# Expert weights in one transfer a tile, with runs of 8 KB for a partition

## What is computed

```python
y = jnp.zeros(xt.shape, dtype=jnp.float32)
for e in range(N_EXPERTS):                                  # 16
    he = jax.nn.silu(xt @ w_gate[e]) * (xt @ w_up[e])       # 1024 -> 512
    y = y + combine[:, e:e + 1] * (he @ w_down[e])          # 512 -> 1024
```

## Time and profile before

| | |
|---|---|
| median of 3 runs | 2187.03 us (2185.16 to 2195.76) |
| span of the profiled execution, its own time | 2187.5 us |
| TensorE busy (matmul) | 1962.1 us, 90% |
| weight loads busy | 1488.9 us, 68% |
| VectorE, ScalarE, GpSimd busy | 746.8, 737.2, 1008.6 us |
| mean granted TensorE clock | 0.944 of full |
| bytes moved by DMA | 477.02 MB, mean 218 GB/s |

### The profile page before, as it was taken

The page is one execution under the profiler, slowest core; times in us unless marked ns, Lnnn a source line. Parts: engine busy times, 40 slices in busy tenths (PEclk is TensorE's granted clock), DMA queues, the critical chain, the costliest instruction groups (busy, mean ns, idle before and its releaser), DMA issues. The chain is left out here.

```text
span 2187.5 us, 29236 instructions
## 1 busy us (share of the span) xinstructions
PE 1962.1 (90%) x11525; PEld 1488.9 (68%) x11525; DVE 746.8 (34%) x1336; ACT 737.2 (34%) x1026; POOL 1008.6 (46%) x784
## 2 busy tenths in 40 slices
PE   7879888999789997999887898999999997887998
PEld 5556654555367774554476686789988997767997
DVE  3453232111433133111244777821163214533112
ACT  3332320011233231111134545544364444444342
POOL 6326500000345630000174284088888886516886
PEclk9979998999899998999997998999999999998999
DMA  7535668999857649999953153056565665304662
GB/s 260 191 115 199 235 253 340 409 409 409 301 205 251 237 169 382 409 409 409 367 167 116 58 184 96 1 155 190 181 181 174 181 190 169 116 10 135 183 185 95
DMA packets 294981, 477.02 MB, mean 218 GB/s; under 512 B 16762, under 2 KB 196973, under 8 KB 294733
## 3 DMA queue, kind: packets, MB, share of 16 engines
q1 hardware_dynamic: 288812, 459.82, 59.5%
q10 hardware_dynamic: 6048, 15.53, 2.0%
HBM read 474.15 MB, written 1.15 MB: 217 GB/s over the span
## 5 line engine op out<-in xcount | busy, mean ns | idle before, releaser
L644 POOL TENSOR_TENSOR w_lo<-raw,w_hi 128x512 fp32r<-128x512 f32 x780 | 1008.4, 1327 | 1162.4 <-ACT w_hi L1426 1162.4
L710 PE MATMUL PS<-at_hi,w_hi 128*128 128x256 f32 x1680 | 488.4, 291 | 20.8 <-DVE at_lo L1935 16.9
L1426 ACT ACTIVATE w_hi<-raw 128x2048 fp32r<-128x2048 f32 x195 | 371.7, 1908 | 344.2 <-PE PS L712 335.8
L711 PE MATMUL PS<-at_lo,w_hi 128*128 128x256 f32 x1680 | 481.2, 286 | 0.0
L712 PE MATMUL PS<-at_hi,w_lo 128*128 128x256 f32 x1680 | 481.1, 286 | 0.0
L710 PEld LDWEIGHTS PS<-at_hi,w_hi 128*128 128x128 f32 x1680 | 328.7, 196 | 35.4 <-DVE at_lo L1935 16.3
L711 PEld LDWEIGHTS PS<-at_lo,w_hi 128*128 128x128 f32 x1680 | 328.7, 196 | 3.7 <-issue 2.6
L712 PEld LDWEIGHTS PS<-at_hi,w_lo 128*128 128x128 f32 x1680 | 328.3, 195 | 0.0
L710 PE MATMUL PS<-w_hi,at_hi 128*128 128x512 f32 (+1 forms) x480 | 192.6, 401 | 31.3 <-DVE at_lo L1935 13.7
L711 PE MATMUL PS<-w_lo,at_hi 128*128 128x512 f32 (+1 forms) x480 | 187.8, 391 | 0.0
L712 PE MATMUL PS<-w_hi,at_lo 128*128 128x512 f32 (+1 forms) x480 | 187.6, 391 | 0.0
(11 more groups left out here) (312 smaller groups left out, 2499.9 us busy)
## 6 DMA issues: line engine op xcount, KB each, us to landing
raw<-ffn_w_gu SPq DMA_DIRECT2D x132, 512.0 KB, 5.0
raw<-ada_w SPq DMA_DIRECT2D x64, 768.0 KB, 5.3
raw<-ffn_w_down SPq DMA_DIRECT2D x66, 512.0 KB, 4.1
raw<-l_e_up SPq DMA_DIRECT2D x48, 512.0 KB, 15.1
raw<-diff_w_in SPq DMA_DIRECT2D x48, 512.0 KB, 4.6
raw<-l_xkv SPq DMA_DIRECT2D x32, 512.0 KB, 5.6
w_plain_hi<-l_e_gate SPq DMA_DIRECT2D x32, 512.0 KB, 15.0
w_plain_lo<-l_e_gate SPq DMA_DIRECT2D x32, 512.0 KB, 15.3
```

The source lines that it names most:

```text
L644: ins = nc.gpsimd.tensor_tensor(w_lo[:, n % RING, part], raw[:, order_of(n) % RAW, part], w_hi[:, n % RING, part].bitcast(F32), ALU.subtract)
L710: pe.matmul(dst, s_hi, m_hi, start=first, stop=False)
L711: pe.matmul(dst, s_hi, m_lo, start=False, stop=False)
L1426: nc.scalar.activation(w_hi[:, n % RING, :], raw[:, s % RAW, :], ACT.Copy).then_inc(hi_done, 1)
```

## The change

One transfer loads a whole tile, and the 128 partitions get 8 KB each in one run: four consecutive rows of gate or up (512 floats each), two of down (1024 floats each). Before, each of two transfers brought a run of 4 KB: two rows of gate or up, one of down. The semaphore's threshold goes from 32 to 16. The chunks of the contraction take the columns of `X` four apart instead of two, and the chunks of the hidden product two apart instead of neighbouring. The branch `experts_all`, for the case that an expert has more than 64 tokens, is changed in the same way.

```diff
-        Xk = X[:, :, :].rearrange("p t (c q i) -> p t c i q", c=4, i=2)
+        hid_f = hid.rearrange("p (h q i) -> p h i q", h=2, i=2)
+        Xk = X[:, :, :].rearrange("p t (c q i) -> p t c i q", c=2, i=4)
+        all_h_f = all_h.rearrange("p (a h q i) -> p a h i q", a=4, h=2, i=2)
...
                     t = moe_slot(at, layer)
-                    for j in range(2):
-                        sp.dma_start(t[:, j * D:(j + 1) * D], rows[j]).then_inc(moe_landed[slot], 16)
+                    sp.dma_start(t, rows).then_inc(moe_landed[slot], 16)
...
-                            load_expert([w[e, (2 * h + j) * 256:(2 * h + j + 1) * 256, :].rearrange("(q i) n -> q (i n)", i=2)
-                                         for j in range(2)])
+                            load_expert(w[e, h * 512:(h + 1) * 512, :].rearrange("(q i) n -> q (i n)", i=4))
...
-                            load_expert([dw[e, (2 * h + j) * P:(2 * h + j + 1) * P, :] for j in range(2)])
+                            load_expert(dw[e, h * 256:(h + 1) * 256, :].rearrange("(q i) n -> q (i n)", i=2))
...
-                    pe.wait_ge(moe_landed[slot], 32 * (layer * in_layer + m // MOE_RING + 1))
+                    pe.wait_ge(moe_landed[slot], 16 * (layer * in_layer + m // MOE_RING + 1))
...
-                            ins = pe.matmul(PS[:, 6 + k // 4, (k % 4) * P:(k % 4 + 1) * P], Xk[:, t, k // 2, k % 2, :],
+                            ins = pe.matmul(PS[:, 6 + k // 4, (k % 4) * P:(k % 4 + 1) * P], Xk[:, t, k // 4, k % 4, :],
                                             onehot_t[:, t, :], start=t == 0, stop=t == NT - 1)
...
-                        ins = pe.transpose(PS[:, 5, j * P:(j + 1) * P], hid[:, j * P:(j + 1) * P], ident[:, :])
+                        ins = pe.transpose(PS[:, 5, j * P:(j + 1) * P], hid_f[:, j // 2, j % 2, :], ident[:, :])
```

More of the change, by code:

```diff
@@ L1220, in experts_all @@
                         for i in range(2):
-                            ins = pe.transpose(PS[:, 4 + j, (2 * i + t) * P:(2 * i + t + 1) * P], Xk[:, t, j, i, :], ident[:, :])
+                            ins = pe.transpose(PS[:, 4 + j, (2 * i + t) * P:(2 * i + t + 1) * P], Xk[:, t, j // 2, 2 * (j % 2) + i, :], ident[:, :])
                 ins.then_inc(g["x_full"], 1)
@@ L1261, in experts_all @@
                             for t in range(NT):
-                                at = (2 * e + t) * 512 + j * P
                                 ins = pe.transpose(PS[:, 4 + 2 * e + j // 2, ((j % 2) * NT + t) * P:((j % 2) * NT + t + 1) * P],
-                                                   all_h[:, at:at + P], ident[:, :])
+                                                   all_h_f[:, 2 * e + t, j // 2, j % 2, :], ident[:, :])
                     ins.then_inc(g["ht_full"], 1)
```

## The result

The changed kernel took 2235.52 us (median of 4 runs, 2233.37 to 2237.3), the kernel before 2189.78 in the same comparison: ratio 1.0216, 95% interval 1.0199 to 1.0233. The change costs about 2 per cent. The profiled execution has a span of 2234.1 us, 46.6 more than before.

The account below looks back on a forecast made before the run. TensorE and the DMA loads were both taken as near their limit in the expert stretches. From 2187.5 us, gather +47.5 and waits -5.2 gave 2229.8, so 2229 against the median; range 2177 to 2236.

Parts of the forecast that it names:

- the +47.5 us of the sum: Gather's weight loads at line 1120: 3.4 us more a gather, 7 gathers in each of 2 layers.
- the first gathers: First gather of each layer, 6.76 us, 0.21 us a record, close to the pace in question: left unchanged.
- the likeliest case: Gather's weight load at its dearest price: 2229 us forecast, own range 2222 to 2236, chance 0.48.
- TensorE and the loads are both close to their limit, the loads behind: Expert stretches: TensorE's own work 28.2 us a pair, the weight loads 30.8 us at 409 GB/s.
- The upper end: Gather's weight load: each column pays what two pay now, streaming 106 to 212 ns, 106 ns more a record.
- The 12 ns to spare: Gather: 106 ns of streaming against 118 ns a record, so the load hides behind the matmul by 12 ns.
- Waits for weights, -5.2: TensorE's waits for expert weights in both layers, 5.2 us in total, would go with faster loads.
- The rate, +2 per cent between nothing and 3.5: Expert weight transfers in 8 KB runs: rate gain taken as some 2 per cent, between none and 3.5.
- the band table's 0.326: Price in us of the trace's only 8 KB packets, against 0.328 for two of 4 KB: no gain.
- Transposes of `hid` and issues, 0: Transposes at line 1165 reading every second column, and 192 fewer issues on SyncE's queue: no cost, no gain.
- That far columns cost nothing: Rival on the gather's loads: distance is free, only the transfers change; 2182 us, at worst 2187, chance 0.32.
- A gain of over 11 us: Rival: more than the waits comes back, needing TensorE time below 28.2 us a pair; chance 0.04.

Follow-up runs that it names:

- the ladder of distances: Kernel before, gather columns 1 apart in layer 0 and 3 in layer 1, then 8 and 6 in a second kernel: 2199.33 and 2233.23 us, one run each.
- the loads alone: Changed kernel with the gather reading every second column of X as before, larger transfers kept: 2185.54 us, ratio 0.9991.
- the columns alone: Kernel before with its 4 KB transfers, the gather alone reading every fourth column of X: 2237.12 us, ratio 1.0229.
- The two kernels with the copy: ScalarE copies X once a layer so the gather reads neighbouring columns: in the changed kernel 2181.68 us, in the kernel before 2190.62 us.

## Where the prediction was right, and which step of it failed

The direction and the mechanism came out as forecast. The step that failed is a price: the weight load of far columns, the +47.5 us of the sum, was put too low, and with it the first gathers, which were put at nothing. 2229 was predicted, 2235.5 measured, at the outer edge of the likeliest case's own range (2222 to 2236; the chances give 2224 to 2236 for the same case). Of the 6.5 us between them, 2.8 lie in the kernel before, which took 2189.78 in this comparison and not the 2187.03 that the forecast starts from. The change itself was put at 47.5 - 5.2 = 42.3 us and measured 45.7 in the medians, 46.6 in the traces; the gathers cost 51.8 + 1.9 = 53.7 us there instead of 47.5.

- *TensorE and the loads are both close to their limit, the loads behind.* Right: with the loads faster TensorE waits no more, with TensorE faster at the old loads it waits 3 us longer.
- *The step that failed: what a load of far columns costs.* The upper end was taken, streaming doubled to 212 ns and a record at 224, the load at about 300. Measured are 234 a record and 328 a load: 3.70 us more a gather instead of 3.4, 14 x 0.3 = 4.2 us. The premise, pieces that hold two of today's columns, is borne out by the ladder of distances, but a piece costs 1.83 ns, and two columns' streaming (2 x 0.83 = 1.66) was put in its place.
- *The 12 ns to spare.* They were read in two ways, as slack of a load hidden behind its matmul and as something to add to 212, and they were neither. Neighbouring columns run at 112 ns a record, so the load at every second column already held the pace at 118 and had nothing to spare; and 128 x 1.83 = 234 needs nothing on top. A piece too cheap and 12 ns too many partly offset each other, so it was partly luck that 224 came so near.
- *The choice of the upper end.* It rested on 6 ns between two kinds of load, with chances of 0.48 against 0.32 for the loads alone. The rows of before could not decide it, and that the likelier case came true is in part luck. "No load gets shorter by reading farther apart" does not hold among far distances: 318 ns at 6, 328 at 4.
- *The first gather of a layer, left as it is.* Wrong by 0.97 us in either layer: 6.76 was "close to the pace in question", but below it.
- *Waits for weights, -5.2.* Right in the traces: none is left. In the medians, where the columns stay as they were, 1.8 us show.
- *The rate, +2 per cent between nothing and 3.5.* Measured 3 per cent (409 to 421 GB/s); 0.315 us a packet agrees with the slope from 2 to 4 KB (0.316, by which the gain is 3.7 per cent and not 3.5), and the band table's 0.326 was the worse guide, perhaps because other traffic shared its engines.
- *Transposes of `hid` and issues, 0.* Right: the transposes' loads grew by 62 ns, but the pair is explained without them, and half the issues changed nothing.
- *The rivals.* That far columns cost nothing falls with the columns alone (2237.12); its 2182 is about what the loads alone give (2185.54). A gain of over 11 us was not seen in the medians of any kernel here.

The two pages that the prediction weighed are told apart. The Trainium skill (Advanced Engine Details and Errata, section SBUF Cachelines) asks for two hits on a line of 16 bytes: distance 2 has two and is nearly free, 3 and 4 have fewer and are not; the traces agree (192 ns for neighbours, then 196, 261, 328). The Trainium skill (SBUF — State Buffer, section Door 1: The DMA port swizzle) lets a stride of four fp32 go free; for TensorE's weight load it doesn't, and the measurement decides.

## What to carry to other kernels

A layout that gives the DMA longer runs moves the stride to whoever reads the tile or its partner: look there for the load with the least slack, and price it by the pieces of 16 bytes that it touches, not by its columns alone. Before a rate is bought, read what there is to win: here the waits were 5 us, however much faster the queue became. Here TensorE and the loads stood within a tenth of each other (28.2 and 30.8 us a pair): relieving either one alone gave nothing clear of the noise, and a copy of 4 us a layer on an idle engine made both pay.

## What the runs showed of the hardware that was not expected

- TensorE's weight load of 128 float32 columns: 192, 196, 261, 328, 318, 334 ns at distances of 1, 2, 3, 4, 6, 8 words; 1.83 ns for each 16 bytes touched from 64 pieces on.
- At a distance of 4 words the gather's pace does not follow TensorE's clock. The rows below lie within gathers of the changed kernel, then of the kernel before; the columns are those of the earlier trace rows, with the granted clock behind the last count in brackets. 4 us at 0.50, the lower level of 1.2 GHz, hold 18 weight loads, and 4 us at 1.00, 2.4 GHz, hold 18 too. Before, at a distance of 2, 4 us at 0.50 hold 21, and 3.7 us at 1.00 hold 32. This is also why the first gathers, which begin at 0.50, lost only 0.97 us.

```profile
340.00:344.00 4.00, 4.00 (x18) 4.00 (x18) 0.00 (x0) 0.00 (x0) 0.00 (x0) 0.50 0.94 391
1056.00:1060.00 4.00, 4.00 (x19) 4.00 (x18) 0.20 (x1) 0.00 (x0) 0.00 (x0) 1.00 1.01 422
...
341.40:345.40 4.00, 4.00 (x21) 4.00 (x21) 0.00 (x0) 0.00 (x0) 0.00 (x0) 0.50 0.94 376
1040.20:1043.90 3.70, 3.70 (x33) 3.70 (x32) 0.69 (x1) 0.00 (x0) 0.00 (x0) 1.00 1.02 407
```

- ScalarE pays for far columns as well. The two kernels with the copy differ in the distance at which it reads `X`: with runs of 8 KB every fourth column, with runs of 4 KB every second. The same function on 128 x 1024 takes 2042 ns in the one and 1125 in the other (min, median, max below).

```profile
L1868 ACT ACTIVATE QT<-X x4: 2023/2042/2052, 325.3 to 831.6; 128x1024 f32<-128x1024 f32 x4
L1869 ACT ACTIVATE QT<-X x4: 1118/1125/1137, 327.1 to 839.9; 128x1024 f32<-128x1024 f32 x4
```
